# Second layer of a two-layer hybrid block: where the wait for the stream's store stands, and how much of the stream is stored

## The reference, cut to what matters

```python
for l in range(DEPTH):                       # DEPTH = 2
    x, xc = hybrid_layer(x, xc, ..., need_ctx=(l < DEPTH - 1))
...
h = x * (1 + scale[:, None]) + shift[:, None]
rk, rv, nk, nv, rq, rg, nq, ng, ch, cb, ccg, cz = split_cols(h @ w_in, PROJ_SPLITS)
...
y = jnp.concatenate([y_conv, y_ret, y_na], axis=-1) @ w_out
x_new = layer_norm(DEEPNORM_ALPHA * x + gate[:, None] * y, ln_g, ln_b)
if not need_ctx:
    return x_new, None
```

## Time and profile before

| | us |
|---|---|
| median of 3 runs | 3355.74 |
| lowest, highest | 3354.76, 3365.66 |
| profiled execution, its own time | 3357.36 |
| its span, first to last instruction | 3355.5 |
| PE busy | 3221.1 (96%) |
| DVE busy | 1538.5 (46%) |
| POOL busy | 1122.4 (33%) |
| ACT busy | 748.9 (22%) |
| mean TensorE clock granted | 0.994 of full speed |

### The profile page before, as it was taken

One profiled execution on the slowest core, in us unless ns is written; L12 is line 12 of the kernel. 1 busy time (PEld: TensorE's weight loads), 2 busy tenths in 40 slices (PEclk: granted clock), 3 DMA queues, 4 the chain that ended last, 5 costly groups with the idle time before them and its releaser, 6 DMA issues.

```text
span 3355.5 us, 41945 instructions
## 1 busy us (share of the span) xinstructions
PE 3221.1 (96%) x17662; PEld 2582.4 (77%) x17662; DVE 1538.5 (46%) x1625; ACT 748.9 (22%) x961; POOL 1122.4 (33%) x525
## 2 busy tenths in 40 slices
PE   6999998999889999899999999999999999999999
PEld 5877876787668788798576788788788888888757
DVE  3134428328822423824766601442553154255476
ACT  1011225112211122511334501112301011001241
POOL 2232220135532232044133344453144344434323
PEclk9999999999999999999999999999999999999999
DMA  6210111332131011112111111112211111111212
GB/s 235 70 32 14 39 35 48 126 137 84 61 119 38 14 38 47 57 42 109 63 51 38 38 44 54 38 54 97 76 49 45 50 50 44 50 50 45 81 44 75
DMA packets 59243, 208.16 MB, mean 62 GB/s; under 512 B 5856, under 2 KB 7648, under 8 KB 59104
## 3 DMA queue, kind: packets, MB, share of 16 engines
q1 hardware_dynamic: 42240, 143.15, 13.3%
q10 hardware_dynamic: 16864, 62.97, 5.0%
HBM read 188.27 MB, written 17.83 MB: 61 GB/s over the span
## 4 chain that ended last, share of the span: by engine, by line
PE 75%; DVE 16%; ACT 5%; DMA 2%; issue 1%; ACTq 0%; DVEq 0%
PE ps L541 65%; DVE Sb L1748 3%; PE ps L800 2%; DMA modfirst<-modw 1%; DVE stage L1839 1%; PE ps L523 1%; PE ps L568 1%; PE ps L710 1%; PE ps L1037 1%; PE ps L625 1%; DVE xc L1970 1%; DVE Y L1834 1%; DMA xin<-xT 1%; PE ps L947 1%; DVE stage L1854 1%
## 5 line engine op out<-in xcount | busy, mean ns | idle before, releaser
L467 POOL TENSOR_TENSOR w_hi<-raw,pool_zero 128x1024 fp32r<-128x1024 f32 (+2 forms) x242 | 454.0, 1876 | 2139.1 <-PE ps L541 2065.7
L469 POOL TENSOR_TENSOR w_lo<-raw,w_hi 128x1024 fp32r<-128x1024 f32 (+2 forms) x242 | 633.4, 2617 | 19.0
L541 PE MATMUL ps<-h_hi,w_hi 128*128 128x512 f32 (+1 forms) x1832 | 491.0, 364 | 26.5 <-ACT QK L1101 15.4
L541 PE MATMUL ps<-g_hi,w_hi 128*128 128x512 f32 x1568 | 490.5, 394 | 10.2 <-DVE g_lo L1574 5.2
L541 PE MATMUL ps<-g_lo,w_hi 128*128 128x512 f32 x1568 | 483.1, 389 | 0.0
L541 PE MATMUL ps<-g_hi,w_lo 128*128 128x512 f32 x1568 | 482.8, 389 | 0.0
L541 PE MATMUL ps<-h_lo,w_hi 128*128 128x512 f32 (+1 forms) x1832 | 469.7, 352 | 0.0
L541 PE MATMUL ps<-h_hi,w_lo 128*128 128x512 f32 (+1 forms) x1832 | 469.4, 352 | 0.0
L541 PEld LDWEIGHTS ps<-h_hi,w_hi 128*128 128x128 f32 x1832 | 301.0, 189 | 100.2 <-issue 23.3
L541 PEld LDWEIGHTS ps<-g_hi,w_hi 128*128 128x128 f32 x1568 | 292.9, 188 | 82.6 <-issue 9.4
L541 PEld LDWEIGHTS ps<-g_lo,w_hi 128*128 128x128 f32 x1568 | 294.4, 188 | 61.5
(11 more groups left out here) (312 smaller groups left out, 3451.2 us busy)
## 6 DMA issues: line engine op xcount, KB each, us to landing
raw<-s SPq DMA_DIRECT2D x226, 512.0 KB, 3.5
modring<-modw ACTq DMA_DIRECT2D x32, 512.0 KB, 4.7
xin<-xT ACTq DMA_DIRECT2D x1, 5120.0 KB, 18.2
x_saved<-Y ACTq DMA_DIRECT2D x1, 5120.0 KB, 16.3
xin<-x_saved ACTq DMA_DIRECT2D x1, 5120.0 KB, 17.6
modfirst<-modw SPq DMA_DIRECT2D x4, 1024.0 KB, 10.8
modfirst<-modw ACTq DMA_DIRECT2D x4, 1024.0 KB, 19.4
x_saved<-Y ACTq DMA_DIRECT2D x1, 4096.0 KB, 11.7
```

The lines of the kernel that those rows point to most:

```text
L467: G.tensor_tensor(w_hi[s][:, :n], raw[s][:, :n], zero.to_broadcast([P, n]), ALU.add).then_inc(hi_done, 1)
L469: G.tensor_tensor(w_lo[s][:, :n], raw[s][:, :n], w_hi[s][:, :n].bitcast(F32), ALU.subtract)\
L541: last = T.matmul(ps[:, o + c0:o + c0 + size], wt[s][:, kk], xx[:, k, t0:t0 + size], start=(x == 0 and n == 0), stop=(x == k_n - 1 and n = ...
```

## The change

Three edits. The wait of ACT for the store moves from ahead of the first copy of layer 1 to ahead of the seventh, the first that writes into the memory of `Y`. The constant products ahead of block c = 4 go from 20 to 8. The store at the end of layer 0 and the load in layer 1 leave out the context columns: 4096 KB each, in pieces of 4 KB with a pitch of 5 KB in DRAM, where it was 5120 KB in one run.

```diff
@@ PE, head of layer 1
-                        keep_busy(2, (10, 0, 1, 0, 20, 0)[c])
+                        keep_busy(2, (10, 0, 1, 0, 8, 0)[c])
@@ ACT, head of layer 1, after the table loads
-                if l:
-                    act.wait_ge(xs_out, 16)
                 skip = 0 if l == 0 else CTX
@@ ACT, behind the copies of the first six blocks
+                if l:
+                    act.wait_ge(xs_out, 16)
                 for c in range(3):
                     evac(g0 + 6 + 2 * c, VT[:, c, :], T1, 3)
@@ ACT, end of layer 0
-                    act.dma_start(x_saved.rearrange("k p t -> p k t"), Y[:]).then_inc(xs_out, 16)
+                    act.dma_start(x_saved.rearrange("k p t -> p k t")[:, :, CTX:], Y[:, :, CTX:]).then_inc(xs_out, 16)
@@ ACT, end of layer 1
-                        act.dma_start(xin[:], x_saved.rearrange("k p t -> p k t")).then_inc(xr_in, 16)
+                        act.dma_start(xin[:, :, CTX:], x_saved.rearrange("k p t -> p k t")[:, :, CTX:])\
+                            .then_inc(xr_in, 16)
```

## The result

| | before | changed |
|---|---|---|
| median us (5 runs each) | 3356.32 | 3340.27 |
| lowest, highest | 3354.76, 3365.66 | 3336.34, 3348.54 |
| profiled execution, its span | 3357.36, 3355.5 | 3348.54, 3346.7 |
| mean clock of the profiled execution | 0.994 | 0.991 |

The ratio is 0.9946, with a 95% interval of 0.9924 to 0.9968: faster by 0.54%, or 18 us; the two medians are 16.05 us apart. The forecast was 3337.9 in a range of 3333 to 3345.

What follows compares the result with a forecast made beforehand. PE's own queue and the places where PE stands still were taken to bound the kernel. 8.40 + 1.87 + 7.56 = 17.8 us off the 3355.74 median gave 3337.9 us, range 3333 to 3345.

Steps and rivals of the forecast that it cites:

- The hole: PE's idle before block c = 2, from ACT's wait for the store: closes when the wait moves, 8.40 us.
- the clock: The granted clock fell in PE's idle before c = 2; c = 2 gets back 1.87 us, bounds 0 and 1.94.
- The constant products: Ahead of c = 4, 20 become 8; they cover nothing, so all 7.56 us come off PE's queue.
- the split's margin: The split of c = 4's weights on POOL ends at 964.4, 6.1 us ahead of PE.
- The smaller transfers: A fifth less to store and to load in layer 1; nobody on the path waits for it: 0 us.
- The narrow place: Weights loaded beside the store: c = 4's land 1.4 us ahead of POOL, c = 5's at 962.8, needed at 965.5.
- inner range: 3335 to 3340 us for the forecast itself, given 78%: clock term 0 to 1.94, scatter of runs about 1 us.
- signs of being wrong: PE idle before c = 2 (ACT) or c = 4 or 5 (POOL), or a stretch behind 1000 us over 1 us longer.
- rival B: The clock falls elsewhere, at later short stalls, once or twice at 1.87 us: 3339.8 or 3341.6 us; 10%.
- Rival D: ACT meets another equally long wait, say stalled table issues; only 7.56 us gained, 3348.2 us; 4%.

Runs made afterwards that it cites:

- the filled hole: The kernel before with 14 constant products ahead of c = 2 where there was 1, wait unmoved: median 3361.66 us, ratio 0.9996 to 1.0019.
- the kernel with three stores: The changed kernel without constant products ahead of c = 4, with two spare whole-stream stores issued ahead of the real one: median 3362.75 us.
- the second set: The changed kernel again, unaltered, in more runs: median 3343.74 us, ratio 0.9944 to before.
- the lag: The changed kernel with no constant products ahead of c = 2 and c = 4, and lag=1 for lag=3 in the first pair: median 3338.55 us.

## Why the prediction was right

**The hole (8.40 us) and the clock (1.87).** Together 10.59 in the kernel with the wait only, against 10.27. By the starts of the rows the hole gave 8.68 and the clock 1.94, just on its upper bound; the filled hole gives the clock 2.0. At full clock c = 2 took 8.62 and 8.63, within the 8.62 to 8.77 of its two likes. The hole came out 0.3 larger because two constant instructions were put at 0.63 us, and c = 2 starts 0.34 behind their first row. Where the wait went, it waits for nothing: the VT copy is released by PE. How deep the clock term goes doesn't follow the length of the hole: c = 2 took 10.60, 10.56, 10.26 and 11.00 us behind holes of 4.57, 8.23, 9.32 and 23.79.

**The constant products (7.56 us).** They gave 7.73 alone and 7.74 in the change (12.60 to 4.86), and nothing was covered. The 0.315 us of one was 12.60 / 40, and the row behind them starts some 0.3 us early; the 24 that came off took 0.32 each. The other 16 came off too, for 5.02 us, as the split's margin said. With these terms the sum is 8.69 + 1.93 + 7.74 = 18.36, and the stretch gives 18.34.

**The smaller transfers (0).** Right in the change, and 3.6 us alone. Read as a list of edits the change would sum to 21.9; the third one only takes from the hole what the first takes whole.

**The narrow place.** The weights of c = 4, changed kernel:

```profile
L417 SPq DMA_DIRECT2D raw<-s x1: 333/333/333, 952.8 to 952.8; - x1
...
DMA to landing us min/median/max: 9.0/9.0/9.0
...
962.73 1.89 POOL L467 TENSOR_TENSOR w_hi<-raw,pool_zero 128x1024 fp32r<-128x1024 f32 x1 [4.60 <-PE ps L541]
```

They landed in 9.0 us, against 8.6 in the trace of before, at 961.8 and so still 0.9 us ahead of POOL. The prediction called c = 5 the narrowest place, but by its own numbers c = 5 had 2.7 us and c = 4 had 1.4; measured it is 3.7 (landing 6.2 us after 958.3, split at 968.21) and 0.9. The Trainium skill, page "DMA: Bandwidth & Descriptors", section "Queues, rings and completion order", has the engines take turns between queues. The traces agree: loads issued while a store was under way landed in 6.7 to 9.5 us, whether there were one, two or three. In the kernel with three stores the second store, queued when c = 4's weights were issued at 949.1, landed only at 973.1, so in line behind it they would have needed some 24 us (an estimate), and they took 8.5.

**The size.** 18.3 us in the stretch and 18 by the ratio, against 17.8. The median of the first five runs is 2.4 us above the forecast, and the profiled one 9.0 above its own forecast of 3339.5. The forecast's own inner range, 3335 to 3340, was missed by 0.27, and one of its signs of being wrong came: the stretch behind 1000 us was longer than before by more than 1 us (the gap, by 4.97). That the median still lies so near is in part luck, since the five runs spread over 12 us and the second set's median is 3343.74; the 18.34 of the stretch is not luck.

What was mis-sized is rival B. The prediction took the scatter for 1 us, from median and lowest, where the highest of its three runs lay 10 us above. It held the mean clock of 0.994 to leave little, but 0.006 of 3355 us is 20 us of full clock (an estimate), and 0.001 more or less goes with 2.3 us. And it priced a fall of the clock at 1.87 us, from the one place that I had looked at; a single place, the first pair of the feed-forward part, has it between 0 and 8.6 us (gaps of 47.32 to 55.95, with two kernels near 47.3 and four near 55.9), and it differs between executions of the same program. That the long fall isn't made by the change is shown: the kernel with the products only, the filled hole and the changed kernel have it, the changed kernel's second profile doesn't, nor does the one with the whole store. What decides it in one execution stays open; I tried only the lag, and it didn't shorten that part (83.84 us against 83.20).

**Rival D** I gave 4%, with the argument that the last issue ended with the store in full flight. The argument held, but by less than I knew: with one more whole store on ACT's queue it fails.

## What to carry to other kernels

When a wait on an engine in order is moved behind work that doesn't need it, count the hole that it leaves in the engine downstream, the clock that the hole costs, and any filler put in since; and don't add up edits that shorten the same wait. Filler products deserve the same test as waits: name what ends last beside them, and if it ends before they begin, they are pure time. Measure a change of 0.5% between two milestones of the profile around the edit, not by the span alone: here, where PE waits for no transfer, the distance between milestones repeated to 0.01 us and the span to 10. And look at the mean clock of every execution before you put a scatter down to the edit.

## What the runs showed that I had not expected

- Issuing a transfer can hold an engine as long as waiting for one. With one whole store (5120 KB, 1024 pieces of 5 KB) already queued and the one of 4096 KB behind it, the next issue on ACT, of only 512 KB, took 12.66 us instead of 0.59; with a third store, two issues took 12.74 and 13.44. Each of them ended some 3 us before the oldest outstanding store landed (956.13 and 958.9; 956.86 and 959.8; 970.33 and 973.1), so room seems to come as that store drains; whether bytes or pieces fill the queue wasn't tested. In the profile it is no wait on a semaphore: the idle reads "issue", and the long row is the DMA instruction itself.
- The stall hits the queue of the engine that issues. SP's loads, issued in the same time, took 0.33 us to issue and 7.3 to 8.6 to land.
- One stretch of unchanged code had four lengths in 13 profiles, near 47.3, 49, 51 and 56 us, with the TensorE clock low for none, part or 20 us of it. Of the changed kernel alone it had two.
